# Both layers of a hybrid decoder trunk written out, and the attention steps of ScalarE and VectorE in another order

## What is computed

```python
h = concatenate([meta, x], axis=1)                    # 272 rows
for l in range(2):
    g = norm_g[l]
    h = h + 0.5 * rmsnorm(swiglu(rmsnorm(h, g[0]), ffn_w_in[l, 0], ffn_w_out[l, 0]), g[1])
    hn = rmsnorm(h, g[2])
    u_pool, q, k, v, gate_pool, gate_attn = split(hn @ w_in[l], SPLITS, axis=-1)
    y_pool = pool_mixer(u_pool, pool_w_grp[l], pool_scale[l], w_pool_proj[l])
    attn = swa_attention(q, k, v, sinks[l])           # 16 heads, 4 key heads, window 128, ALiBi, sinks
    y_attn = attn @ w_attn_proj[l]
    merged = sigmoid(gate_pool) * y_pool + sigmoid(gate_attn) * y_attn
    h = h + rmsnorm(merged @ w_o[l], g[3])
    h = h + 0.5 * rmsnorm(swiglu(rmsnorm(h, g[4]), ffn_w_in[l, 1], ffn_w_out[l, 1]), g[5])
return h[:, 16:]
```

## Time and profile before

| | |
|---|---|
| median of three runs | 1295.85 us |
| the profiled execution's own time | 1295.62 us |
| its span, first to last instruction | 1293.7 us |
| TensorE busy | 1237.7 us (96%) |
| VectorE busy | 744.0 us (58%) |
| ScalarE busy | 530.7 us (41%) |
| GpSimd busy | 451.3 us (35%) |
| mean granted clock of TensorE | 0.982 of full speed |
| moved by DMA | 197.12 MB, mean 152 GB/s |

### The profile page before, as it was taken

How to read it: one execution, slowest core, us unless ns; L and a number is a source line. 1 busy time by engine, 2 the same in 40 slices (tenths; PEclk the granted TensorE clock), 3 DMA queues, 4 the chain that set the end, 5 groups by cost and what they waited for, 6 DMA issues and landing times.

```text
span 1293.7 us, 26538 instructions
## 1 busy us (share of the span) xinstructions
PE 1237.7 (96%) x9877; PEld 1209.2 (93%) x9877; DVE 744.0 (58%) x1034; ACT 530.7 (41%) x738; POOL 451.3 (35%) x529
## 2 busy tenths in 40 slices
PE   6999999999899999999969999997988999999998
PEld 5999999898899999999969999997987999999997
DVE  5555444757776665544456554447577866655443
ACT  5333334435564443333424333334355644444241
POOL 2645410304412355541016455012043123655401
PEclk9899999899999999999989999998999998999999
DMA  8554457262166365445716543574421672654440
GB/s 272 186 171 154 134 158 232 83 193 81 50 151 211 97 214 176 154 134 156 235 40 196 180 157 125 169 215 135 137 81 50 155 237 68 226 194 164 137 155 33
DMA packets 203158, 197.12 MB, mean 152 GB/s; under 512 B 4168, under 2 KB 202032, under 8 KB 203072
## 3 DMA queue, kind: packets, MB, share of 16 engines
q1 hardware_dynamic: 202784, 195.69, 48.5%
q10 hardware_dynamic: 288, 0.27, 0.1%
HBM read 194.90 MB, written 1.05 MB: 151 GB/s over the span
## 4 chain that ended last, share of the span: by engine, by line
PE 71%; issue 13%; DVE 7%; ACT 5%; POOL 4%; DMA 0%; DVEq 0%; POOLq 0%; ACTq 0%; SPq 0%
PE bank L393 23%; PE bank L395 22%; PE bank L394 22%; ACT w_hi L714 3%; POOL rt L1309 2%; PE bank L475 1%; POOL acc L1305 1%; DVE s L1125 1%; DVE tmp L976 1%; DVE stats L1129 1%; DVE x_lo L955 1%; DVE h L985 1%; POOL acc L1302 1%; ACT sq L724 1%; DVE gates L1084 0%
## 5 line engine op out<-in xcount | busy, mean ns | idle before, releaser
L393 PE MATMUL bank<-x_hi,w_hi 128*128 128x272 f32 (+1 forms) x2048 | 598.9, 292 | 20.3 <-DVE x_lo L955 10.1
L395 PE MATMUL bank<-x_hi,w_lo 128*128 128x272 f32 (+1 forms) x2048 | 591.8, 289 | 0.0
L904 DVE TENSOR_TENSOR w_lo<-raw,w_hi 128x2048 fp32r<-128x2048 f32 (+2 forms) x205 | 424.8, 2077 | 289.9 <-ACT w_hi L714 289.8
L394 PE MATMUL bank<-x_lo,w_hi 128*128 128x272 f32 (+1 forms) x2048 | 590.3, 288 | 0.0
L714 ACT ACTIVATE w_hi<-raw 128x2048 fp32r<-128x2048 f32 (+2 forms) x216 | 356.8, 1658 | 506.5 <-PE bank L395 496.5
L393 PEld LDWEIGHTS bank<-x_hi,w_hi 128*128 128x128 f32 x2048 | 391.3, 191 | 23.6 <-DVE x_lo L955 11.6
L394 PEld LDWEIGHTS bank<-x_lo,w_hi 128*128 128x128 f32 x2048 | 390.9, 191 | 0.3
L395 PEld LDWEIGHTS bank<-x_hi,w_lo 128*128 128x128 f32 x2048 | 390.8, 191 | 0.0
L393 PE MATMUL bank<-hid_hi,w_hi 128*128 128x272 f32 (+1 forms) x704 | 201.5, 286 | 0.0
L394 PE MATMUL bank<-hid_lo,w_hi 128*128 128x272 f32 (+1 forms) x704 | 201.3, 286 | 0.0
L395 PE MATMUL bank<-hid_hi,w_lo 128*128 128x272 f32 (+1 forms) x704 | 200.9, 285 | 0.0
(11 more groups left out here) (157 smaller groups left out, 1137.2 us busy)
## 6 DMA issues: line engine op xcount, KB each, us to landing
raw<-in_ffn_w_in SPq DMA_DIRECT2D x88, 1024.0 KB, 5.0
raw<-in_ffn_w_out SPq DMA_DIRECT2D x32, 768.0 KB, 4.4
raw<-in_w_in SPq DMA_DIRECT2D x24, 1024.0 KB, 5.5
raw<-in_ffn_w_out SPq DMA_DIRECT2D x32, 640.0 KB, 4.1
raw<-in_w_in SPq DMA_DIRECT2D x16, 512.0 KB, 5.1
raw<-in_w_attn_proj SPq DMA_DIRECT2D x32, 256.0 KB, 4.6
raw<-in_w_o SPq DMA_DIRECT2D x8, 1024.0 KB, 7.9
raw<-in_w_pool_proj SPq DMA_DIRECT2D x8, 512.0 KB, 3.4
```

Source lines behind the costliest of these rows:

```text
L393: pe.matmul(ps[:, t0:T], w[0], a_hi[:, t0:T], start=start, stop=False)
L394: pe.matmul(ps[:, t0:T], w[0], a_lo[:, t0:T], start=False, stop=False)
L395: return pe.matmul(ps[:, t0:T], w[1], a_hi[:, t0:T], start=False, stop=stop)
L904: last = dve.tensor_tensor(lo, w, hi.bitcast(F32), ALU.subtract)
```

## The change

The layer loop is written out on all five engines: the layer's number is now known when the program is made, so TensorE's two branches by layer, the loop's return, and the branches by layer on ScalarE and VectorE are gone, and the semaphore values outside the remaining loops are constants. The feed-forwards' inner loops stay. In the attention steps ScalarE makes the high split first, takes tanh of the two gate tiles of the step before behind it, and then goes on as before; VectorE makes the low split first, and takes the attention output behind the inversion of the first sum. In layer 1 everything for the queries of the meta tokens is left out, on all engines. The core of the diff:

```diff
+def meta_queries(l):
+
+    return l < DEPTH - 1
...
-            with sp.Fori(0, DEPTH) as l:
+            for l in range(DEPTH):
...
                 if f == 0:
-                    with pe.If(l < 1):
+                    if l < 1:
                         pair_in_turn(*first_pair)
-                    with pe.Else():
+                    else:
                         deep_pair(*first_pair)
...
                 unit(U_POOL, l, T_POOL, (2, 3), 2, KD, x_hi, x_lo)
-                scores0(l)
+                if meta_queries(l):
+                    scores0(l)
...
-                    if c == META_STEP:
+                    if c == META_STEP and meta_queries(l):
                         attend_meta(l)
...
-                pe.wait_ge(o_meta_ready, l + 1)
+                if meta_queries(l):
+                    pe.wait_ge(o_meta_ready, l + 1)
...
-            with pe.Fori(0, DEPTH) as l:
+            for l in range(DEPTH):
                 ffn(0, l)
 
                 deep_pair(U_K, l, x_hi, x_lo, lambda k: x_tile(KD + k, l), lambda: sum_squares(2, l))
                 spread_rms(2, l)
-                with pe.If(l < DEPTH - 1):
+                if l < DEPTH - 1:
                     after_kv(l, 0)
-                with pe.Else():
+                else:
                     after_kv(l, META)
...
-                    with act.If(l < DEPTH - 1):
+                    if l < DEPTH - 1:
                         split_hi(0, l + 1)
...
-                act.wait_ge(s0_step, l * S0_STEPS + S0_SHIFTED)
-                act.activation(s0[0:META, :, 0:META], s0[0:META, :, 0:META], ACT.Exp)
-                act.activation(stats0[:, 2, :], stats0[:, 1, :], ACT.Exp).then_inc(s0_exp, 1)
+                if meta_queries(l):
+                    act.wait_ge(s0_step, l * S0_STEPS + S0_SHIFTED)
+                    act.activation(s0[0:META, :, 0:META], s0[0:META, :, 0:META], ACT.Exp)
+                    act.activation(stats0[:, 2, :], stats0[:, 1, :], ACT.Exp).then_inc(s0_exp, 1)
                 for c in range(KD):
-                    tanh(2 * c, l)
+                    split_hi(49 + c, l)
                     if c >= 1:
+                        tanh(2 * c - 2, l)
+                        tanh(2 * c - 1, l)
                         take_pT(2 * c - 2, l)
                     exps(2 * c, l)
                     exps(2 * c + 1, l)
                     if c >= 1:
                         take_pT(2 * c - 1, l)
-                    tanh(2 * c + 1, l)
-                    split_hi(49 + c, l)
                 split_hi(57, l)
+                tanh(2 * KD - 2, l)
+                tanh(2 * KD - 1, l)
                 take_pT(HEADS - 2, l)
...
-                softmax0_shift(l)
+                if meta_queries(l):
+                    softmax0_shift(l)
                 split_lo(48, l)
                 take_pool(1, l)
                 for c in range(KD):
+                    split_lo(49 + c, l)
                     take_gate_tile(2 * c, l)
-                    if c >= 2:
-                        take_o(c - 2, l)
                     bias_and_max(2 * c, l)
                     bias_and_max(2 * c + 1, l)
                     invert_sum(2 * c, l)
+                    if c >= 2:
+                        take_o(c - 2, l)
                     if 1 <= c <= GROUPS:
                         take_z(c - 1, l)
-                    if c == 0:
+                    if c == 0 and meta_queries(l):
                         softmax0_sum(l)
-                    if c == 1:
+                    if c == 1 and meta_queries(l):
                         softmax0_scale(l)
-                    if c == META_STEP:
+                    if c == META_STEP and meta_queries(l):
                         take_o_meta(l)
                     take_gate_tile(2 * c + 1, l)
                     invert_sum(2 * c + 1, l)
                     if c < GROUPS:
                         mix(c, l)
-                    split_lo(49 + c, l)
                 split_lo(57, l)
```

More of the change, by code:

```diff
@@ L830, in _ @@
                 square(0, k, h[:, k, :], h_ready, k + 1)
-            with act.Fori(0, DEPTH) as l:
+            for l in range(DEPTH):
                 ffn(0, l)
@@ L1044, in ffn @@
                 else:
-                    with dve.If(l < DEPTH - 1):
+                    if l < DEPTH - 1:
                         split_lo(0, l + 1)
@@ L1049, in ffn @@
                     mean_square(5, l)
-                    with dve.If(l < DEPTH - 1):
+                    if l < DEPTH - 1:
                         split_lo_between(2, l + 1, lambda: boundary(2, l, l * 4 * KD + 4 * KD, g_next))
-                    with dve.Else():
+                    else:
                         last_update(l)
@@ L1146, in take_o @@
                 dve.tensor_copy(o_hi[:, c, META:T], o_bank[:, META:T]).then_inc(ohi_ready, 1)
-                dve.wait_ge(ohi_ready, l * (KD + 1) + c + 1 + (c > META_STEP - 2))
+                dve.wait_ge(ohi_ready, l * (KD + 1) + c + 1 + (meta_queries(l) and c > META_STEP - 2))
                 dve.tensor_tensor(o_lo[:, c, META:T], o_bank[:, META:T], o_hi[:, c, META:T].bitcast(F32), ALU.subtract
@@ L1206, in _ @@
             split_lo(2, 0)
-            with dve.Fori(0, DEPTH) as l:
+            for l in range(DEPTH):
                 layer_columns(l)
@@ L1358, in normalise @@
                 last.then_inc(p_ready, 1)
-            with pool.Fori(0, DEPTH) as l:
+            for l in range(DEPTH):
                 ffn(0, l)
```

## The result

The changed kernel takes **1258.65 us** (median of 4 runs, 1258.39 to 1260.2), the kernel before 1295.9 us in the same comparison: a ratio of 0.9727, with a 95% interval of 0.9713 to 0.974. The forecast was 1263.4 us, with a range of 1257 to 1271. The profiled execution's own time is 1260.2 us, its span 1258.1 us, 35.6 us shorter than the span before.

The account below looks back on a forecast made before the run. TensorE was busy 1237.7 of 1293.7 us, leaving at most 56 us; a ring of ScalarE and VectorE bound the attention steps. Jump terms 17.9 + attention terms 14.3 = 32.2 us off 1295.6 gave 1263.4 us, range 1257 to 1271.

Parts of the forecast that it names:

- (a): Layer change, scale spread to scale spread: 30.15 us against 18.77 at a boundary without a jump, so 11.4 us to win.
- (b): Jump to layer 1's copy, ahead of its query products: 5.5 us idle plus 2.4 us of half clock, 7.9 us.
- (c): Half clock may return at the two repaired places, nothing to 3.2 us each: 1.4 us taken off for both.
- ring, layer 0: Attention steps of layer 0: the shortened ring of 9.54 us removes all TensorE idle time there, 5.7 us.
- ring, layer 1: Attention steps of layer 1: ring 0.14 us too long in each of five steps, so 7.1 of 7.8 us go.
- (d): Layer 1's meta queries: their score (0.50 us) and attention (1.04 us) products leave TensorE, 1.5 us.
- The ring: ScalarE and VectorE work that closes each attention step without idle time, 10.67 us; moving two pieces out leaves 9.54 us.
- the two holes: TensorE idle 9.79 us at 663.36 and 5.50 us at 899.47, put down to far jumps of its sequencer.
- the ring stays too long: Rival: in the attention steps the new order loses half its 1.13 us on VectorE; 1269.6 us, chance 0.15.
- the holes stay: Rival: TensorE waits there for something else and branches are only recorded across it; 1281.3 us, chance 0.04.
- the remaining loops begin to miss: Rival: return jumps of the feed-forward loops come to cost about 4 us each; 1324 us, chance 0.03.

Follow-up runs that it names:

- writing out alone: Changed kernel with the layers written out, but ScalarE and VectorE steps in the old order and meta queries kept in both layers: 1275.08 us against 1294.54.
- the repetition: The changed kernel run again with no edit: 1258.46 us.
- the other run with all three: The kernel before with only the two edits of order on ScalarE and VectorE, layer loop and far jumps kept: 1283.08 us against 1294.54.

## Why the prediction was right

The changed profile shows each step at its place. With the traces of all runs:

| term | forecast | measured | from |
|---|---|---|---|
| (a) layer change | 11.4 | 11.5 | 30.15 to 18.66 |
| (b) jump to layer 1's copy | 7.9 | 8.2 | 189.55 to 181.37, writing out alone |
| (c) half clock coming back at the two repaired places | -1.4 | -1.6 | 874.6, in this execution; 174.78 against 173.18 in the repetition |
| ring, layer 0 | 5.7 | 6.2 | 188.34 to 182.18; 0.4 of it came with writing out alone |
| ring, layer 1 | 7.1 | 5.9 | 181.37 to 175.47 |
| (d) meta queries | 1.5 | 2.3 | 175.47 to 173.18 |
| sum | 32.2 | 32.5 | |

**(a), (b).** That a boundary of the same program without a jump gives the price was the safest step, and it held to 0.1 us. That jumps were the cause is shown by writing out alone. The finer reading, 3.28 + 4.60 + 3.27 us by branch, was wrong as a sum of parts: taking one of 3.27 us away gave 2.1, or 1.1 against the other run with all three. Only the whole could be priced.

**(c).** The match of 1.4 and 1.6 is luck. The forecast was a guess between 0 and 6.4 us, and in the repetition of the same kernel the half clock came at neither of the two places.

**The ring.** 9.54 us were forecast. The order alone is worth 188.34 - 182.18 - 0.4 = 5.8 us in layer 0, since writing out gave 0.4 without it; the forecast had given the register instructions nothing, with up to 2 us in the range. The step shown of layer 0 has 9.75 = 1.94 + 2.56 + 3.23 + 2.02: the high split, the low split and gate tile, two heads until the exponential at 324.87, exponential and copy. All pieces but one are those of the earlier trace rows to 0.02 us; the two heads took 3.23 us instead of 3.03. In layer 1 steps of 9.52 and 9.76 us alternate. Each of its two removed pieces, put back alone, brought steps of 10.2 to 11 us. In layer 1, TensorE's own step was taken too long (9.40 us, the period less the wait that is shown): the wait left of 0.30 us in a ring of 9.52 says 9.22 us. In the step that the forecast used, the products up to the second turning of weights (L558) took 985.86 - 979.93 = 5.93 us with no idle time shown, and the same products in the changed kernel 945.29 - 939.47 = 5.82; so 0.11 of the 0.18 us was, it seems, a wait that the modelled ends of the products hide. The waits left are 0.92, 0.30, 0.54 and 0.26 us, 2.0 in all, where 0.7 was forecast. That is, to 0.1 us, the 1.2 us by which this term was too large.

**(d)** was too small by 0.8 us. 0.3 us of it is waiting in the ring of the first steps, which goes as well; 0.2 us each come at the scores and at the attention, which cost more than the busy time of their products that the forecast took. The last 0.1 us is half clock at the stretch's end in the run with them.

**Where the last 3 us come from.** The spans differ by 35.6 us, the terms make 32.5. The rest is half clock at places the change leaves alone: 1.5 at the head of layer 0, 1.6 at the next boundary, 0.9 at the last one, less 0.3 at one in between and 0.6 at start and tail. The forecast named this as what the lower end of its range was for, with about 3 us. It does not belong to the change's mechanisms in these executions: the kernel with meta queries has the same program up to layer 1's attention and up to there the same half clock as before, and its profiled execution reaches that place 875.01 - 872.75 = 2.3 us later. The average says the same. In the two comparisons that had both kernels, the medians differ by 1295.9 - 1258.65 = 37.3 us and 1294.54 - 1258.46 = 36.1 us, rather than 32.5. The record has the mean granted clock of every execution, in the second comparison 0.982 to 0.984 before (median 0.983) and 0.992 to 0.995 after (0.9935). An estimate from these: 2 x 0.017 x 1292.6 = 44 us at half clock before and 2 x 0.0065 x 1256.5 = 16 us after, 28 us less, of which the two holes' stretches are 20.5. The other 7 us are worth up to 3 us of time. Why the changed kernel gets them stays open; the kernel that is only written out does not have them (0.988 to 0.99).

**The rivals.** That the ring stays too long came true in the small: waits of 2.0 us were left in layer 1 and of 0.2 us in layer 0. That the holes stay was refuted by writing out alone. That the remaining loops begin to miss did not happen (0.235 us at most), and writing them out as well changed nothing. The Trainium skill gives 51 and 108 ns for branches ("Advanced Engine Details and Errata", Control Flow Timing); the second is about half of what the loops' return jumps took here (0.21 us in the median), and both fail for the far ones by a factor of 30 and more.

## What to carry to other kernels

Look at the sequencer's branch records when an engine stands still and its data is long ready: far jumps cost this kernel 11.5 us at one place, where three follow each other, and 8.2 us at another, half clock included, and a short loop's return nothing. DMA packets of the kind "instruction" inside the standstill confirm it. When waits of about a microsecond recur on one engine in every step, add up one period around the engines it waits for; if the pieces fill the period without idle time, only moving a piece out of that ring helps, and any engine's idle time inside the period is where it can go. Price a repaired place by a stretch of the same trace that does the same work without the fault, rather than by adding up the parts of the fault.

## What the runs showed of the hardware

- A far jump stopped TensorE's sequencer for 3.2 to 6.6 us, and the stop can appear between two neighbouring instructions behind the jump (3 us, at 655.6 in the kernel with one jump less), with one DMA packet of instructions in it.
- TensorE's granted clock fell to 1.2 GHz around the scale spreads, where it has sums of squares, warming products and idle stretches of 0.6 to 1.6 us, in some executions of a program and not in others. It stayed there for 3.4 or 6.8 us, once for 10.2 us (at 1051.4, with both tanh ahead of the split), and 3.4 us of it cost 1.5 us in the dense feed-forward and 0.4 us at a boundary. It could begin ahead of the idle stretch (at 228.8 before the change; the stretch ended at 229.62), so the idle time alone is not shown to be the cause. Around the holes of 8.6 to 9.9 and 5.3 to 5.9 us it fell in all three kernels that had them, for 10.2 us. More warming products took nearly all of it away, in the profiled executions of the two kernels that had them.
- The same VectorE instructions for two heads took 3.03 us in one step and 3.23 us in another; where the ring is as long as TensorE's own step, that decides whether it waits. What slows them was not tried.
